# The low parts of 144 weight tiles by an adding transfer instead of a GpSimd subtraction

## The reference

```
h = rmsnorm(x) * norm_g
u_a, z_a, u_b, z_b, q, z_x, g_a, g_b, g_x = split(h @ w_in)
o_a = glu(gelu(s5_scan(u_a))) * silu(z_a) @ w_br_ssm
o_b = silu(layernorm(causal_conv31(glu(u_b)))) * silu(z_b) @ w_br_conv
o_x = cross_attention(q, 256 memory tokens) * silu(z_x) @ w_br_xatt
x   = x + (sigmoid(g_a)*o_a + sigmoid(g_b)*o_b + sigmoid(g_x)*o_x) @ w_out
```

## Time and profile before

| | |
|---|---|
| median of 3 runs | 1282.24 us (1277.93 to 1284.35) |
| profiled execution | 1282.3 us, span of its instructions 1280.5 us |
| TensorE (PE) busy | 1171.2 us, 91% |
| VectorE (DVE) busy | 833.8 us, 65% |
| ScalarE (ACT) busy | 397.9 us, 31% |
| GpSimd (POOL) busy | 393.3 us, 31% |
| mean granted TensorE clock | 0.940 |
| moved by DMA | 137.9 MB |

### The profile page before, as it was taken

How to read it: one execution, slowest core, us unless ns; L and a number is a source line. 1 busy time by engine, 2 the same in 40 slices (tenths; PEclk the granted TensorE clock), 3 DMA queues, 4 the chain that set the end, 5 groups by cost and what they waited for, 6 DMA issues and landing times.

```text
span 1280.5 us, 19964 instructions
## 1 busy us (share of the span) xinstructions
PE 1171.2 (91%) x8322; PEld 1074.6 (84%) x8322; DVE 833.8 (65%) x1229; ACT 397.9 (31%) x558; POOL 393.3 (31%) x183
## 2 busy tenths in 40 slices
PE   5999899896897998999799998999998799899995
PEld 4499778596887998899786998787998799889995
DVE  1879776959688852356854796668777896434322
ACT  4332443141242412233123235231322342222212
POOL 0134232222422231244230542232352313214440
PEclk8999998998997997999899998899998889799998
DMA  7563216742212154354323732357422114342442
GB/s 201 168 211 117 83 51 197 131 91 66 81 38 66 43 132 67 96 161 151 98 83 99 247 94 88 100 166 126 98 82 65 50 50 123 66 100 88 133 133 67
DMA packets 205808, 137.94 MB, mean 108 GB/s; under 512 B 45842, under 2 KB 186570, under 8 KB 204934
## 3 DMA queue, kind: packets, MB, share of 16 engines
q1 hardware_dynamic: 205574, 135.61, 38.2%
q10 hardware_dynamic: 144, 1.05, 0.2%
HBM read 121.86 MB, written 15.72 MB: 107 GB/s over the span
## 4 chain that ended last, share of the span: by engine, by line
PE 59%; DVE 31%; DMA 3%; issue 2%; ACT 2%; SPq 2%; POOL 1%; DVEq 0%; ACTq 0%
PE acc L646 40%; DVE cacc L1374 10%; PE acc L687 4%; DVE X L1368 3%; DVE t L1368 2%; PE acc L991 2%; PE mp L898 2%; PE mp L611 2%; DVE cv L1368 1%; PE mp L701 1%; PE mp L816 1%; PE mp L865 1%; PE mp L841 1%; PE mp L808 1%; SPq L500 1%
## 5 line engine op out<-in xcount | busy, mean ns | idle before, releaser
L566 POOL TENSOR_TENSOR w_lo<-w_st,w_hi 128x1024 fp32r<-128x1024 f32 x144 | 371.1, 2579 | 833.4 <-ACT w_hi L1078 833.0
L646 PE MATMUL acc<-h_hi,w_hi 128*128 128x260 f32 x1664 | 349.1, 292 | 5.3 <-DVEq L1721 5.3
L646 PE MATMUL acc<-h_lo,w_hi 128*128 128x260 f32 x1664 | 339.7, 286 | 0.0
L646 PE MATMUL acc<-h_hi,w_lo 128*128 128x260 f32 x1664 | 339.5, 286 | 0.0
L1078 ACT CAST w_hi<-w_st 128x1024 fp32r<-128x1024 f32 x144 | 150.9, 1048 | 604.6 <-PE acc L646 565.0
L646 PEld LDWEIGHTS acc<-h_hi,w_hi 128*128 128x128 f32 x1664 | 263.6, 193 | 14.0 <-issue 8.3
L646 PEld LDWEIGHTS acc<-h_hi,w_lo 128*128 128x128 f32 x1664 | 262.1, 193 | 0.0
L646 PEld LDWEIGHTS acc<-h_lo,w_hi 128*128 128x128 f32 x1664 | 261.3, 192 | 0.0
L1374 DVE SCALAR_TENSOR_TENSOR cacc<-vx,cw,cacc 128x512 f32<-128x512 f32 x232 | 205.7, 955 | 4.0 <-DVE xT L1368 2.1
L646 PE MATMUL acc<-bh,w_hi 128*128 128x260 f32 x384 | 82.6, 298 | 18.4 <-POOL w_lo L566 8.3
L1368 DVE TENSOR_TENSOR sg<-acc,sg 128x520 f32<-128x520 f32 x32 | 22.4, 699 | 90.3 <-PE acc L646 88.0
(11 more groups left out here) (280 smaller groups left out, 1488.4 us busy)
## 6 DMA issues: line engine op xcount, KB each, us to landing
w_st<-in_w_in SPq DMA_DIRECT2D x104, 512.0 KB, 3.9
kb<-in_cache_mem_k SPq DMA_DIRECT2D x16, 512.0 KB, 5.6
kb<-in_cache_mem_v SPq DMA_DIRECT2D x16, 512.0 KB, 4.2
w_st<-in_w_out SPq DMA_DIRECT2D x16, 512.0 KB, 4.1
x_scratch<-xT SPq DMA_DIRECT2D x8, 520.0 KB, 7.1
xT<-x_scratch SPq DMA_DIRECT2D x4, 1040.0 KB, 8.0
kvw<-in_w_k SPq DMA_DIRECT2D x8, 512.0 KB, 6.6
kvw<-in_w_v SPq DMA_DIRECT2D x8, 512.0 KB, 3.7
```

The costliest lines, as they stand in the source:

```text
L566: pool.tensor_tensor(w_lo[:, n % 2, :], w_st[:, n % 2, :], w_hi[:, n % 2, :].bitcast(F32), ALU.subtract).then_inc(w_staged_free, 1)
L646: last = pe.matmul(acc_ps[acc][:, a, 0:HC], w_of(w, slot, k), x_of(x, k, a), start=(k == 0 and p == 0), stop=(k == kts - 1 and p == 2))
```

## The change

ScalarE now writes two copies of a unit: first the negative one, rounded, to `w_lo`, then the rounded one to `w_hi`. GpSimd issues a DMA from `w_st` to `w_lo` that adds while it writes, so that `w_lo` becomes `w_st` minus the rounded value. A unit can be used for the high by high products when `w_hi` is there; TensorE waits for the adding transfer of the slot only ahead of the other two kinds of product, so `products` now runs over k twice. A slot is loaded again when `w_hi` is made and the adding transfer has landed.

Five pieces of order are moved as well: in the attention the turned probabilities of block 0 come ahead of the scores of block 1 (and ScalarE keeps them ahead of its exponentials of block 1); the transposes of the last convolution rows (`v_last`, `v_s`) come behind the gates and branches 6 and 7 of gx, and ScalarE's copy of them likewise; the first two gb loads come ahead of SP's wait for that copy; and VectorE makes the second layer's `powers` and `level_factors` behind the first sums of the output product instead of ahead of them.

```diff
@@ SP
             def ring_load(l, src, i, width=P):
                 n = l * UNITS + i
-                sp.wait_ge(w_staged_free, n + 1)
+                if n >= 2:
+                    sp.wait_ge(w_hi_done, n - 1)
+                    sp.wait_ge(w_lo_done[n % 2], 16 * (n // 2))
                 sp.dma_start(w_st[:, n % 2, :].rearrange("p (k c) -> p k c", c=width), src).then_inc(w_loaded[n % 2], 16)
...
+                gate_loads(l, "gb", 0, 2)
                 wait(sp, l, "vs_ev", 1)
...
-                gate_loads(l, "gb", 0, 12)
+                gate_loads(l, "gb", 2, 12)
@@ GpSimd
-                        pool.wait_ge(w_hi_done, n + 1)
-                        pool.tensor_tensor(w_lo[:, n % 2, :], w_st[:, n % 2, :], w_hi[:, n % 2, :].bitcast(F32),
-                                           ALU.subtract).then_inc(w_staged_free, 1)
+                        pool.wait_ge(w_neg_done, n + 1)
+                        pool.dma_start(w_lo[:, n % 2, :], w_st[:, n % 2, :], accum_op=ALU.add).then_inc(w_lo_done[n % 2], 16)
@@ TensorE
+            def products(l, n, acc, name, i, high, low, kts, w_of, tiles_done=None):
+
+                pe.wait_ge(w_hi_done, n + 1)
                 wait(pe, l, f"acc_free{acc}", use[name] + i + 1)
                 for k in range(kts):
                     if tiles_done:
                         wait(pe, l, tiles_done, k + 1)
-                    for p, (w, x) in enumerate(terms):
+                    for a in range(2):
+                        pe.matmul(acc_ps[acc][:, a, 0:HC], w_of(w_hi, n % 2, k), high[:, k, a, :], start=(k == 0), stop=False)
+
+                pe.wait_ge(w_lo_done[n % 2], 16 * (n // 2 + 1))
+                for k in range(kts):
+                    for w, x in ((w_lo, high), (w_hi, low)):
                         for a in range(2):
-                            last = pe.matmul(acc_ps[acc][:, a, 0:HC], w_of(w, slot, k), x_of(x, k, a),
-                                             start=(k == 0 and p == 0), stop=(k == kts - 1 and p == 2))
+                            last = pe.matmul(acc_ps[acc][:, a, 0:HC], w_of(w, n % 2, k), x[:, k, a, :],
+                                             start=False, stop=(k == kts - 1 and w is w_hi))
                 last.then_inc(acc_ready[acc], 1)
...
+                turn_probabilities(0)
                 scores(1)
-                turn_probabilities(0)
@@ ScalarE
                     act.wait_ge(w_loaded[n % 2], (n // 2 + 1) * 16)
+                    act.activation(w_lo[:, n % 2, :], w_st[:, n % 2, :], ACT.Copy, scale=-1.0).then_inc(w_neg_done, 1)
                     act.copy(w_hi[:, n % 2, :], w_st[:, n % 2, :]).then_inc(w_hi_done, 1)
...
+                keep_probabilities(0)
                 exps(1)
-                keep_probabilities(0)
@@ VectorE
                 merge("ga", 3)
-                if l + 1 < LAYERS:
-                    powers(l + 1)
-                    level_factors(l + 1, 0, 1)
...
                         if i == 0:
-                            level_factors(l + 1, 1, 3)
+                            powers(l + 1)
                         elif i == 1:
+                            level_factors(l + 1, 0, 3)
+                        elif i == 2:
                             level_factors(l + 1, 3, 5)
-                        elif i == 2:
+                        elif i == 3:
                             scaled_inputs(l + 1)
```

More of the change, by code:

```diff
@@ L230, in build @@
         w_loaded = [sem(f"w_loaded{i}") for i in range(2)]
-        w_staged_free = sem("w_staged_free")
+        w_lo_done = [sem(f"w_lo_done{i}") for i in range(2)]
         w_hi_done = sem("w_hi_done")
+        w_neg_done = sem("w_neg_done")
         dve_steps = sem("dve_steps")
@@ L558, in _ @@
                                pattern=[[-1, P]], channel_multiplier=1).then_inc(sm["consts"], 1)
-            pool.sem_inc(w_staged_free, 2)
             for l in range(LAYERS):
@@ L636, in state_parameters @@
                 last.then_inc(sm["c_tr"], 1)
-            def products(l, slot, acc, name, i, terms, kts, x_of, w_of, tiles_done=None):
+            def products(l, n, acc, name, i, high, low, kts, w_of, tiles_done=None):
+                pe.wait_ge(w_hi_done, n + 1)
                 wait(pe, l, f"acc_free{acc}", use[name] + i + 1)
@@ L651, in tile_w @@
                 return w[:, slot, k * P:(k + 1) * P]
-            def tile_x(x, k, a):
-                return x[:, k, a, :]
             def in_unit(l, name, i, tiles_done=None):
                 n = l * UNITS + unit[name] + i
-                pe.wait_ge(w_staged_free, n + 3)
-                products(l, n % 2, i % 2, name, i // 2, ((w_hi, h_hi), (w_lo, h_hi), (w_hi, h_lo)), KT, tile_x, tile_w, tiles_done)
+                products(l, n, i % 2, name, i // 2, h_hi, h_lo, KT, tile_w, tiles_done)
             def gate(l, name, j):
                 n = l * UNITS + unit[name] + j // 2 * 3 + j % 2
-                pe.wait_ge(w_staged_free, n + 3)
-                products(l, n % 2, j % 2, name, j // 2 * 2, ((w_hi, h_hi), (w_lo, h_hi), (w_hi, h_lo)), KT, tile_x, tile_w)
+                products(l, n, j % 2, name, j // 2 * 2, h_hi, h_lo, KT, tile_w)
             def branch(l, name, j, ready):
                 n = l * UNITS + unit[name] + j // 2 * 3 + 2
-                pe.wait_ge(w_staged_free, n + 3)
                 low = {"gx": q_r[:, :, :, :], "gb": cv_r[:, :, 0, :, 0:HC], "ga": q_r[:, :, :, :]}[name]
-                high = bh[:, :, :, :]
-                products(l, n % 2, j % 2, name, j // 2 * 2 + 1, ((w_hi, high), (w_lo, high), (w_hi, low)), ET, tile_x,
+                products(l, n, j % 2, name, j // 2 * 2 + 1, bh[:, :, :, :], low, ET,
                          lambda w, slot, k: w[:, slot, (k * 2 + j % 2) * P:(k * 2 + j % 2 + 1) * P], ready if j == 0 else None)
@@ L919, in _ @@
                 branch(l, "gx", 5, "br_x_done")
+                gate(l, "gx", 6)
+                gate(l, "gx", 7)
+                branch(l, "gx", 6, "br_x_done")
+                branch(l, "gx", 7, "br_x_done")
                 wait(pe, l, "v_last_done", 4)
@@ L928, in _ @@
                 last.then_inc(sm["vs_tr"], 1)
[L929 to L932, removed]
                 in_unit(l, "zb", 0)
@@ L1007, in _ @@
                     n = l * UNITS + unit["out"] + i
-                    pe.wait_ge(w_staged_free, n + 3)
-                    products(l, n % 2, i % 2, "out", i // 2, ((w_hi, m_hi), (w_lo, m_hi), (w_hi, m_lo)), KT, tile_x, tile_w,
+                    products(l, n, i % 2, "out", i // 2, m_hi, m_lo, KT, tile_w,
                              "m_done" if i == 0 else None)
@@ L1267, in _ @@
                 branch("gx", 2)
+                gate("gx", 6)
+                gate("gx", 7)
+                branch("gx", 3)
                 wait(act, l, "vs_tr", 2)
@@ L1270, in _ @@
                 act.copy(nrow[32:32 + NB, :], mp[0:NB, 0, :]).then_inc(sm["vs_ev"], 1)
-                gate("gx", 6)
-                gate("gx", 7)
-                branch("gx", 3)
                 silu("zb", 0, q)
```

## The result

| | before | after |
|---|---|---|
| median of 4 runs | 1282.85 us (1277.93 to 1284.35) | 1297.08 us (1294.9 to 1300.83) |
| ratio to before, 95% interval | | 1.0121 (1.0086 to 1.0155) |
| span of the profiled execution | 1280.5 us | 1293.6 us |
| mean granted TensorE clock | 0.940 | 0.954 |

The change makes the kernel 1.2% slower. The time lies inside the predicted range, but on the other side of no change than the forecast of 1238 us.

What follows compares the result with a forecast made beforehand. TensorE, busy for 91%, was taken as the bound, with the gain in its waits, most ending with VectorE. Gains of 81 us and costs of 38 gave 1282 - 81 + 38 = 1239, say 1238 us; range 1197 to 1312.

Steps and rivals of the forecast that it cites:

- a to d: Waits on VectorE, w_lo, powers and probabilities go: 30 + 8.3 + 9.1 + 7.2 = 54.6 us; better clock 26; gain 81.
- (g): Adding transfer, issue to landing taken as 6.0 us: only the branches stall, 24 x 0.5 = 12 us cost.
- (h): DMA load of the adding transfers, 2.6 us each: 13 us cost, in 555 to 590 and 85 to 125 us and the like.
- a landing time over 7.5 us makes the prediction wrong in sign: Sign for the adding transfer: past 7.5 us ring-bound costs, 26 + 50 x (T - 6.4), reach the 81 us gain.
- the ring-bound rival: Transfer time over 6.4 us makes a slot's round outlast two units: 80 us at 8.0, giving 1307 us; chance 0.24.
- VectorE's time doesn't reach TensorE: Rival: VectorE, freed of one wait, meets the next and the clock stays; 24.6 us come, 38 go: 1295; chance 0.12.
- (f): ScalarE's added copy with a factor, 1.05 us each, mostly hidden: four chains where TensorE waits get 1 us longer, 4 us cost.
- (i): New product order inside a unit leaves more matmuls behind the last tile where tiles come one by one: 6 us cost.
- (k): Path over y_scratch to the GLU shares the DMA engines with adding transfers: 1.5 us a layer, 3 us cost.
- SP is not what those waits end with, nothing: Moving the gb loads ahead of SP's wait was priced at no gain.
- GpSimd in VectorE's way: Rival: issuing a transfer may wait for a VectorE instruction, 0.74 us; 32 us more, 1270 us; chance 0.06.
- the short transfer: Rival: adding transfer takes up to 5 us, no branch stalls and the DMA engines don't fill up: 1214 us; chance 0.16.

Runs made afterwards that it cites:

- e3: Changed kernel with a plain copy from w_st to w_lo instead of the adding transfer (outputs wrong): 1240.72 us, ratio 0.9663 to the kernel before.
- e6: e1 with ScalarE's negative copy put back, GpSimd adding instead of subtracting: 1293.3 us, ratio 1.0062 to the kernel before.
- e1: Changed kernel with GpSimd's subtraction back for the adding transfer and negative copy, new product order and moves kept: 1282.66 us, ratio 0.9996 to the kernel before.
- e7: e1 with the old product order as well, so only the moves are left: 1271.13 us, ratio 0.9892 to the kernel before.
- e2: Changed kernel with the old product order, each unit waiting for its low part before its first matmul: 1336.84 us, ratio 1.0407 to the kernel before.
- e11: Changed kernel with the second layer's parameter rows issued ahead of the load of ga 5: 1298.46 us, ratio 1.014 to the kernel before.
- e5: Changed kernel with the adding transfer only in gx 3 to gb 11 (50 units), subtraction elsewhere: 1254.97 us, ratio 0.9788 to the kernel before.
- e9: e5 with unit v 3 of each layer taking the adding transfer too: 1270.51 us, ratio 0.9917 to the kernel before.
- e8: Changed kernel with the transfer adding 512 of 1024 columns and GpSimd adding the others: 1299.45 us, ratio 1.0121 to the kernel before.

## Why the prediction was wrong

**The gain (a to d) was nearly right.** The five rows on VectorE stood at 32.8 us. After the change L1843 has 4.3, L1722 0.5 and X 1.3, so 26.7 of the 30 came. With the 8.3 of `w_lo`, the 9.1 of the powers and the 7.2 of the probabilities that is 51.3 us of waits against 54.6 forecast. The clock went from 0.940 to 0.954: 0.046 x 1294 = 60 us are lost at the lower level instead of 77, a gain of 17 where I said 26. That makes 68 us, not 81.

**The step that failed is (g), together with (h): what the adding transfer makes TensorE wait.** They were 12 + 13 = 25 us, and the row is 54.0: 27.0 in the branches, where I had 12, and 27.0 in the other units, where I had nothing. The typical duration wasn't at fault: 5.5 us in the median is better than the 6.0 I took, and by my own limits (5.5 in a branch, 6.5 in a full unit) it should have cost nothing. The limits weren't at fault either: in six of the branch waits the wait is T less 5.3 us each time, for a T of 6.3 to 9.9. What failed is that one duration was held against a limit, where the landings go from 4.5 to 10.0 us, 39 of the 144 take over 6.5, and each late one costs its excess, while an early one gives nothing back. The landings of 9.9 and 10.0 us in ga both had the load of 1,040 KB beside them. For the same reason the sign "a landing time over 7.5 us makes the prediction wrong in sign" failed: the median is 5.5, and the sign was wrong.

Bandwidth was priced nearly right: 32.0% of the span is 2.9 us of all engines for each transfer, against the 2.6 of (h). But I charged it only in the stretches that were full already. It made queues form elsewhere: ga was at 0.31 and is at 0.69, with 8.3 us of stalls in the branches from 1125 us on. In 85 to 125 I worked out 41 us of work in 40 and yet charged 4; TensorE lost 8.6. In 555 to 590 I expected a share near 1 and there is 0.77, probably since TensorE, waiting, asks for less.

e3 shows the size: with one read instead of two, and the rest as it is, the kernel takes 1240.72 us. That this is within 3 us of my forecast is partly luck, since (f) and (i) were too small as well. The Trainium skill (Collectives: The Full Stack, The bandwidth ceiling) says that an add needs two source reads, and here the measured time of the engines is 1.9 times that of the copy, which agrees. The time that I worked out with its help, an estimated 4.4 us, was the landing of the fastest transfers only (4.5).

**The range held by luck.** It reached up to 1312 us for the ring-bound rival (1307 us), whose 80 us were to come from a T over 6.4 us in nearly every unit, and the median is 5.5. The loads did come late, though. ScalarE's waits before the negative copy:

```profile
ACT w_lo L1078 <- DMA w_st<-in_w_in: 157.9, 24, 12.6
ACT w_lo L1078 <- DMA w_st<-in_w_out: 30.8, 6, 6.3
```

Before the change the first of them was 38.6 us, in 7 waits. Part of this is only TensorE's lateness seen from ScalarE. What reached TensorE is the five waits of 12.4 us, in three of which (3.9 us) the transfer itself was not slow at all. The rival nearest to the time, "VectorE's time doesn't reach TensorE" (1295 us), had the wrong reason: the gains came, and the new waits ate them.

**(f) was mis-sized:** 4 us forecast, 10.6 measured (e6 against e1, give or take some 6). The copy's duration was right (1060 ns), but what follows it, the evacuation that frees an accumulator, may be late more often than four chains would have it: e6's wait for L1214 is 7.9 us where e1 has 5.6. The rest of the 10.6 is in no single row.

**(i) was mis-sized:** 6 us forecast, 12 measured beside the subtraction (e1 against e7). Beside the transfer the question doesn't arise, since e2 shows that without the new order the change would be 40 us slower still.

**(k) and what I priced at nothing.** The path to the GLU is 5.8 us longer (10.0 against 4.2), not 3. The loads of `kb` land late: those of the value cache, which TensorE waits for, in 6.4 us instead of 4.2, and there is a wait of 4.7 us where 0.2 was. The parameter rows, late on SP, make a wait of 7.1 us; e11 shows that taking it away gains nothing, as others take its place. "SP is not what those waits end with, nothing" was true of the trace of before and not of a ring whose loads wait for a landing.

**The sum with the measured terms:** 1282 - 51 - 17 + 54 + 10.6 + 5.8 + 4.7 + 6 (i) = 1295, against 1297. The terms come from different kernels and overlap a little, and the 6 of (i) is the forecast's: with the 12 that was measured beside the subtraction it would be 1301. That the sum closes so well is partly luck. Of the rivals, GpSimd in VectorE's way is excluded: the convolution's longest multiply-add took 756 ns, GpSimd issued each transfer in 0.85 to 1.08 us, and VectorE was less busy beside the slowest landings than beside the fastest (37% against 65%). The Trainium skill (SBUF - State Buffer, Summary: rules for kernel authors) warns of starved descriptor making beside VectorE; neither the issues nor the landings of this trace show it. That the gains don't arrive is excluded by the waits, and the short transfer (T up to 5) by the median of 5.5 us.

## What to carry to other kernels

Where a transfer replaces an instruction on a path with little slack, price the spread of its landings and not its median: look for the large transfers that can fall beside it, and use it only in the stretches where the engine it relieves is the late one (with the moves, in 50 of the 144 units and with the product order fitted to them it gave 3.1%, where the moves alone gave 1.1%; in all units it lost 1.2%). A transfer that adds costs the DMA engines almost twice the time of a copy of the same bytes. An order of products that hides a late operand should be used only for the units whose operand is late.

## What the hardware did that I had not expected

- The hold between GpSimd and VectorE goes both ways. In the earlier trace rows a VectorE operation on 16 columns lasts as long as GpSimd's subtraction. In e5 a subtraction lasts 15.54 us, until a row of VectorE multiply-adds has ended; in e9 11.00. Both end 2.2 us after the row. Other subtractions inside such a row took 2.9 (e5) and 2.7 us (e9). What decides who is held stays open.
- A transfer of 512 KB inside SBUF landed in 2.8/3.3/9.0 us (minimum, median, maximum) as a copy and in 4.5/5.5/10.0 when it adds, the slow ones beside other DMA traffic. 256 KB added landed in 3.5 us in the median (e8).
- Moving one unit of each layer, 2 of the 144, from a GpSimd instruction to a transfer (e9 against e5) cost 16 us, 1.3%. TensorE's waits on `w_lo` name about 3 of them; what the rest is stays open.
